# Where the sums of the next 512 rows are made and split, and eight reorderings around it, in a two-layer retention and window-attention kernel

## The reference

```python
# layer 0: retention, 4 heads, qk 256 wide, v and gate 512 wide, chunks of 64 rows
h = x @ w_in; q, k, v, g = split(h); q, k = rope(q), rope(k) * 256 ** -0.5
att = einsum(q, k) * decay_mask; inner = att @ v
cross = (q @ state) * xi; state = state * g_chunk + (k * zeta).T @ v
r = normalise(inner + cross)                      # per head, over 512
x = post_norm(x, (silu(g) * r) @ w_out)           # z = alpha * x + out, LayerNorm
# layer 1: window attention, 16 heads of 64, 4 shared key/value heads
k, v = split(x @ w_kv); q, gate = split(x @ w_in)
sc = q @ k.T * 64 ** -0.5 + bias_table[bucket]    # 64 queries against 128 keys
m = max(sc.max(-1), sink); p = exp(sc - m)
p = p / (p.sum(-1) + exp(sink - m)); o = p @ v
x = post_norm(x, (o * silu(gate)) @ w_out)
```

## Time and profile before

| | us |
|---|---|
| median of three runs | 2528.77 |
| the profiled execution, whole | 2527.57 |
| its span, first to last instruction | 2525.5 |
| PE busy in it | 2357.0 (93%) |
| DVE, ACT, POOL busy | 1901.5, 1115.1, 387.7 |
| granted PE clock, mean share of full | 0.972 |

### The profile page before, as it was taken

How to read it: one execution, slowest core, us unless ns; L and a number is a source line. 1 busy time by engine, 2 the same in 40 slices (tenths; PEclk the granted TensorE clock), 3 DMA queues, 4 the chain that set the end, 5 groups by cost and what they waited for, 6 DMA issues and landing times.

```text
span 2525.5 us, 30597 instructions
## 1 busy us (share of the span) xinstructions
PE 2357.0 (93%) x11506; PEld 1913.7 (76%) x11506; DVE 1901.5 (75%) x2693; ACT 1115.1 (44%) x1306; POOL 387.7 (15%) x376
## 2 busy tenths in 40 slices
PE   6799989899999999989999999998999999999995
PEld 5577777777778888777777888777777888878774
DVE  6787878768886668866797766884789667787577
ACT  2333444334544445523544444442454445553353
POOL 4122111132101110021200011102120110010032
PEclk9799999999999999989999999999999999999998
DMA  8776766571554444743274544574246344464413
GB/s 297 258 277 243 252 237 229 188 261 56 196 186 151 130 137 165 260 134 115 75 243 130 165 150 133 165 261 142 67 142 224 98 145 159 125 199 125 136 54 114
DMA packets 211602, 430.77 MB, mean 171 GB/s; under 512 B 14656, under 2 KB 52048, under 8 KB 207872
## 3 DMA queue, kind: packets, MB, share of 16 engines
q1 hardware_dynamic: 195648, 356.70, 43.5%
q0 software_dynamic: 15808, 72.12, 7.9%
HBM read 373.45 MB, written 51.12 MB: 168 GB/s over the span
## 4 chain that ended last, share of the span: by engine, by line
PE 59%; DVE 18%; issue 10%; DMA 7%; ACT 4%; POOL 2%; SPq 1%; POOLq 0%; DVEq 0%; ACTq 0%
PE accs L624 16%; PE accs L625 15%; PE accs L626 15%; DVE w_lo L1211 5%; DMA stage<-t_prep 3%; PE bank L624 3%; PE bank L626 2%; PE bank L625 2%; ACT w_hi L921 2%; DMA stage<-ret_w_in 2%; DMA t_prep<-t_buf 1%; PE bank L838 1%; PE bank L857 1%; PE bank L847 1%; DMA stage<-swa_w_in 1%
## 5 line engine op out<-in xcount | busy, mean ns | idle before, releaser
L1211 DVE TENSOR_TENSOR w_lo<-stage,w_hi 128x1024 fp32r<-128x1024 f32 x536 | 667.2, 1250 | 434.6 <-ACT w_hi L921 426.9
L921 ACT ACTIVATE w_hi<-stage 128x1024 fp32r<-128x1024 f32 x536 | 562.7, 1056 | 626.7 <-DMA stage<-t_prep 277.9
L624 PE MATMUL accs<-w_hi,xs 128*128 128x512 f32 x1120 | 449.3, 401 | 44.1 <-DVE w_lo L1211 11.9
L626 PE MATMUL accs<-w_hi,xs 128*128 128x512 f32 x1120 | 441.3, 394 | 0.0
L625 PE MATMUL accs<-w_lo,xs 128*128 128x512 f32 x1120 | 441.1, 394 | 0.0
L624 PEld LDWEIGHTS accs<-w_hi,xs 128*128 128x128 f32 x1120 | 213.2, 190 | 98.8 <-issue 43.8
L1763 POOL TENSOR_TENSOR rstd<-ve,half 128x1 f32<-128x1 f32 x96 | 80.7, 841 | 1264.2 <-DVE ve L1252 1216.4
L624 PE MATMUL accs<-x_hi,w_hi 128*128 128x512 f32 (+1 forms) x640 | 248.7, 389 | 17.8 <-DVE kT L1624 17.8
L626 PEld LDWEIGHTS accs<-w_hi,xs 128*128 128x128 f32 x1120 | 213.1, 190 | 46.0
L625 PEld LDWEIGHTS accs<-w_lo,xs 128*128 128x128 f32 x1120 | 213.5, 191 | 42.3
L625 PE MATMUL accs<-x_lo,w_hi 128*128 128x512 f32 (+1 forms) x640 | 240.0, 375 | 0.0
(11 more groups left out here) (185 smaller groups left out, 3940.1 us busy)
## 6 DMA issues: line engine op xcount, KB each, us to landing
stage<-t_prep SPq DMA_DIRECT2D x224, 512.0 KB, 4.5
stage<-ret_w_in SPq DMA_DIRECT2D x96, 512.0 KB, 3.9
stage<-ret_w_in SPq DMA_DIRECT2D x128, 256.0 KB, 2.9
stage<-swa_w_in SPq DMA_DIRECT2D x64, 512.0 KB, 4.1
t_prep<-t_buf POOLq DMA_DIRECT2D x28, 1024.0 KB, 8.0
stage<-ret_w_out SPq DMA_DIRECT2D x48, 512.0 KB, 3.6
cs<-rope_t SPq DMA_DIRECT2D x16, 1024.0 KB, 7.4
t_buf<-ret_w_in POOLq DMA_DIRECT2D x32, 512.0 KB, 9.9
```

Source lines behind the costliest of these rows:

```text
L624: mm(dst, lhs[0], rhs[0], start=start, stop=False, skip_group_check=reopened)
L626: return mm(dst, lhs[1], rhs[0], start=False, stop=stop, skip_group_check=reopened)
L921: copy(w_hi[:, g % HS], stage[:, g % LS], ACT.Copy).then_inc(w_hi_made, 1)
L1211: nc.vector.tensor_tensor(w_lo[:, g % LS], stage[:, g % LS], w_hi[:, g % HS].bitcast(F32), sub).then_inc(w_split, 1)
```

## The change

All four sums of the next block are now loaded by POOL as before (`load_part`, RO+15 to RO+24), but added by DVE at the end of pair KV, split by ACT and DVE at pairs Q0 to Q0+3 (`next_sum_hi`, `next_sum_lo`) and stored by SP as hi and lo, two DMAs for each sum, at Q0+1 to Q0+4. At pair 0 of the next block SP loads the eight halves straight into `xs`; nothing is split in head 0 any more (but in block 0). Beside that:

- the key copies stand at KV+2 instead of KV+3, and ahead of `make_hi`/`make_lo` of two pairs;
- two LayerNorm tiles are interleaved (`ln_two_tiles`), at RO+24 ahead of that pair's `make_lo`; at KV-1 `make_lo` follows `turn_x1_lo(0)`; the sums of P4 move from KV-1 to KV;
- the state of the last head is updated half before the statistics, and PE turns tile 1 of it in the middle of pair RO+4;
- in so, `output_sums` stands ahead of `split_so` (up to SO+8);
- scores are negated (query scale, bias and sinks times -1): DVE takes the minimum, ACT does exp(-x + lowest) as four instructions of 128x129, each with its own bias and a running sum, in place of one of 128x516; DVE's subtraction of the maximum and its row sums go;
- the spread of the bias table by DMA moves from ahead of the loop to pair 30; six sets of weight sums are loaded and made later in `T_PLAN`.

```diff
-T_PLAN = [(0, 0, -1, 1), (1, 1, -1, 1), (2, 2, -1, 2), (3, 3, -1, 2), (4, 0, 6, 9), (5, 1, 6, 11), (6, 2, 7, 13),
+T_PLAN = [(0, 0, -1, 1), (1, 1, -1, 1), (2, 2, -1, 2), (3, 3, -1, 2), (4, 0, 8, 11), (5, 1, 9, 13), (6, 2, 10, 14),
...
+                    if s > 0 and p == 0:
+                        sp.wait_ge(products, used(s * NP - 1))
+                        wait_sums_stored(sp, s)
                         for n in range(4):
-                            sp.dma_start(x_sums_next[:, n], x_sums_dram[n]).then_inc(sums_loaded[n], 16)
+                            for hl in range(2):
+                                sp.dma_start(xs[:, X_SUM_SLOT[n], hl].bitcast(F32), x_sums_dram[n, hl])\
+                                    .then_inc(sums_loaded[n], 16)
+                    if s + 1 < NS and Q0 + 1 <= p <= Q0 + 4:
+                        n = p - Q0 - 1
+                        sp.wait_ge(sums_split, 4 * s + n + 1)
+                        if s > 0:
+                            sp.wait_ge(sums_loaded[n], 32 * s)
+                        sp.dma_start(x_sums_dram[n, 0], sum_hi[n % 2][:].bitcast(F32))\
+                            .then_inc(sums_stored[n % 2], 16)
+                        sp.dma_start(x_sums_dram[n, 1], parts_lo[SUM_PART[n]][:].bitcast(F32)).then_inc(sums_stored[n % 2], 16)
...
+                    if p == RO + 4 and j == 0:
+                        turn_r(RH * s + RH - 1, 1)
+                    pe.wait_ge(state_ready, 8 * H + 7)
+                if t == 2:
                     pe.wait_ge(state_ready, 8 * (H + 1))
...
-                        turn_r(H - 1, 1)
                         turn_r(H - 1, 2)
...
+            def next_sum_hi(s, n):
+
+                act.wait_ge(parts_summed, s + 1)
+                if n == 0:
+                    act.wait_ge(scored, 16 * (s + 1))
+                if n > 1:
+                    act.wait_ge(sums_stored[n % 2], 64 * s + 32)
+                copy(sum_hi[n % 2][:], parts[SUM_PART[n]][:], ACT.Copy).then_inc(sums_hi, 1)
...
                 act.wait_ge(turned, 4 * H + t + 1)
                 copy(rT[:, 4 * h:4 * h + 4, t * P:(t + 1) * P],
...
-                    if p == KV + 3:
-                        act.wait_ge(products, full(s, p, 0))
+                        act.wait_ge(products, full(s, KV + 3, 0))
...
                         make_hi(g + AHEAD)
+                        make_hi(g + AHEAD + 1)
+                    if s + 1 < NS and Q0 <= p < Q0 + 4:
+                        next_sum_hi(s, p - Q0)
...
-                            act.wait_ge(p_shifted, NU * s + k + 1)
+                            act.wait_ge(lowest_ready, NU * s + k + 1)
+                            need(act, p_inv, NU * s + k)
+                            for i in range(4):
+                                scores = pr[:, k % 3, i, 0:BAND + 1]
+                                exped = copy(scores, scores, ACT.Exp, bias=lowest[:, i:i + 1], scale=-1.0,
+                                             accum_out=rsum[:, i:i + 1])
+                            exped.then_inc(p_exped, 1)
...
+            def sum_parts(s):
+
+                dve.wait_ge(parts_loaded, 64 * (s + 1))
+                a11, s3, a12, s2 = (x[:] for x in parts)
+                link(nc.vector.tensor_tensor(s3, a11, s3, sub))
+                link(nc.vector.tensor_tensor(s2, s2, s3, sub))
+                nc.vector.tensor_tensor(a11, s2, a11, add)
+                nc.vector.tensor_tensor(a12, a12, s2, sub).then_inc(parts_summed, 1)
+
+            def next_sum_lo(s, n):
+
+                dve.wait_ge(sums_hi, 4 * s + n + 1)
+                nc.vector.tensor_tensor(parts_lo[SUM_PART[n]][:], parts[SUM_PART[n]][:],
+                                        sum_hi[n % 2][:].bitcast(F32), sub).then_inc(sums_split, 1)
...
+            def ln_two_tiles(s, w, t):
+
+                dve.wait_ge(gb_loaded, 32 * (2 * s + w + 1))
+                ln_begin(s, w, t)
+                ln_gain(t)
+                ln_begin(s, w, t + 1)
+                ln_bias(s, w, t)
+                ln_gain(t + 1)
+                ln_bias(s, w, t + 1)
...
-                link(nc.vector.tensor_reduce(mx[:], x[:, :, 0:BAND + 1], AX.X, ALU.max))
-                nc.vector.tensor_tensor(x[:, :, 0:BAND + 1], x[:, :, 0:BAND + 1],
-                                        mx[:].unsqueeze(2).to_broadcast([P, 4, BAND + 1]), sub).then_inc(p_shifted, 1)
+                    link(nc.vector.tensor_scalar(x[:, :, 0:CHUNK], x[:, :, 0:CHUNK], -NEG_INF, None, add))
+                nc.vector.tensor_reduce(lowest[:], x[:, :, 0:BAND + 1], AX.X, ALU.min).then_inc(lowest_ready, 1)
...
             def softmax_back(s, u):
-                link(nc.vector.tensor_reduce(rsum[:], x[:, :, 0:BAND + 1], AX.X, add))
...
-                                split_x_sum(s, 3)
-                        if s > 0 and h == 0 and v in (1, 2, 4, 6):
...
                     if p == KV - 1:
                         turn_x1_lo(s, 0)
-                    if RO <= p < KV:
+                        make_lo(g + AHEAD)
+                    if RO <= p < KV - 1:
                         output_sums(s, "ro", p)
                     if p == RO + 24:
-                        ln_tile(s, 0, 0)
+                        ln_two_tiles(s, 0, 0)
+                        make_lo(g + AHEAD)
                     if p == KV:
                         turn_x1_lo(s, 1)
-                        ln_tile(s, 0, 2)
-                        ln_tile(s, 0, 3)
+                        output_sums(s, "ro", KV - 1)
+                        ln_two_tiles(s, 0, 2)
...
                         turn_x1_lo(s, 3)
+                        if s + 1 < NS:
+                            sum_parts(s)
...
-                    if p == KV + 3:
-                        dve.wait_ge(products, full(s, p, 1))
+                    if p == KV + 2:
+                        dve.wait_ge(products, full(s, KV + 3, 1))
...
                         make_lo(g + AHEAD)
+                        make_lo(g + AHEAD + 1)
+                    if s + 1 < NS and Q0 <= p < Q0 + 4:
+                        next_sum_lo(s, p - Q0)
...
+                    if SO <= p < SO + 9:
+                        output_sums(s, "so", p)
                     for n in SO_SPLITS.get(p, ()):
                         split_so(s, n)
...
-                    if SO <= p:
+                    if SO + 9 <= p:
...
+            def load_part(s, n):
-                for n, (u, i) in enumerate(((0, 0), (0, 1), (1, 0), (1, 1))):
-                    pool.dma_start(parts[n][:], x_turned[:, 4 * u:4 * u + 4, s * SB + i * HT:s * SB + (i + 1) * HT])\
-                        .then_inc(parts_loaded, 16)
+                wait_sums_stored(pool, s - 1)
+                u, i = divmod(n, 2)
+                pool.dma_start(parts[n][:], x_turned[:, 4 * u:4 * u + 4, s * SB + i * HT:s * SB + (i + 1) * HT])\
+                    .then_inc(parts_loaded, 16)
...
-            pool.wait_ge(bias_copied, 1)
-            pool.dma_start(bias_rep.rearrange("(h q n) -> h q n", q=CHUNK, n=NREL),
-                           brow[:].unsqueeze(1).to_broadcast([HEADS, CHUNK, NREL])).then_inc(bias_spread, 16)
...
+                    if p == 30 and s == 0:
+                        pool.wait_ge(bias_copied, 1)
+                        pool.dma_start(bias_rep.rearrange("(h q n) -> h q n", q=CHUNK, n=NREL),
+                                       brow[:].unsqueeze(1).to_broadcast([HEADS, CHUNK, NREL])).then_inc(bias_spread, 16)
...
-                        if p == RO + 18:
-                            load_parts(s + 1)
-                        if p == Q0:
-                            sum_parts(s + 1)
-                        if p == Q0 + 2:
-                            store_sums(s + 1)
+                        if p in (RO + 15, RO + 18, RO + 21, RO + 24):
+                            load_part(s + 1, (p - RO - 15) // 3)
```

148 lines of the change are left out of this document (73 added, 75 removed), and 2 rows, old and new, of the table T_PLAN.

## The result

The changed kernel took 2480.76 us (median of 4 runs, 2479.94 to 2483.47) against 2525.87 for the kernel before (4 runs, 2521.13 to 2528.85): a ratio of 0.9823, 95% interval 0.9804 to 0.9843. The forecast was 2474 in a range of 2450 to 2502. The direction and the size were right to 7 us; the sum was right partly because errors of its terms cancel.

What follows compares the result with a forecast made beforehand. The prediction took PE as the bound in the long stretches, with recurring waits and half-speed clock windows after long ones. Its terms summed to -54.3 us, giving 2474 us in a range of 2450 to 2502.

Steps and rivals of the forecast that it cites:

- Head 0: Head 0 of blocks 1 to 3: PE's 4.82 us wait for att_lo becomes two shorter ones, -9.6 us in all.
- no wait over 3 us: Sign for the profile after: in head 0 PE has no wait over 3 us, two of about 2.
- LayerNorm and kv: Pair 99 and kv: interleaved tiles bring x_lo earlier, -7.4 us in blocks 1 to 3 and -2.7 in block 0.
- predicted waits for w_lo of pair 99: Pair 99: PE newly waits about 2 us (1.3 to 2.1) for weights now made behind the LayerNorm tiles.
- First q pairs: First q pairs: earlier key copies end PE's wait for kT, 24.1 us gone and 4 given back, -20.1 us.
- what is late next are the key moves: First attention step: behind SP's stores the key moves cost PE 1 us in blocks 1 and 2, 2 in block 0.
- at nothing: DVE's four additions and the part_lo splits in q pairs cost nothing; without cover up to +1 us per block.
- so: The so stretches: output_sums ahead of one split shortens PE's waits for z, -4.5 us.
- Softmax: Attention gates: DVE's saved work hides under PE and ACT's four small exps fit its free time, 0 us.
- 0.75 us for each small exp: Attention gates: the limit up to which ACT's free time absorbs the four small exps at no cost.
- Start of block 0: Start of block 0: moving the bias spread and weight sums ends waits for w_lo and att_lo, -10 us.

Runs made afterwards that it cites:

- loads_spread: The changed kernel with the eight loads of half sums spread, two at each of pairs 0 to 3, instead of all at pair 0; ratio 0.9795.
- keys_only: The kernel before with only the key copies of ACT and DVE moved to KV+2, ahead of the weights of two pairs; 2515.32 us, ratio 0.9963.
- w99_first: The changed kernel with DVE's w_lo of pair 99 back ahead of the two interleaved LayerNorm tiles; 2489.15 us, ratio 0.9860.
- qt_first: The changed kernel with ACT's and DVE's qT copies ahead of the last split of the sums instead of behind it; 2476.41 us.
- more_exps: The changed kernel with eight more small exps on ACT per attention unit, results unused, ahead of the four; 2633.54 us, ratio 1.0432.

## Why the prediction was right, and where it was not

**Head 0** (forecast -9.6). Measured -13.6 in head 0. The mechanism held at each step: loads of 1.29 us each, weights late, a new wait at krT, att_lo early, the clock back. Its price was off: the two new waits were 1.4 each in blocks 1 and 2, not 2.3 and 1.7, and left no low clock at all behind them, where half was kept. In block 3 krT was 4.11, against the sign "no wait over 3 us", with a granted clock of 0.65 behind it. loads_spread shows the delay of the eight loads to be worth 1.4, 1.8 and 4.9 us.

**LayerNorm and kv** (-10.1). Measured -8.1 in pair 99 and kv: -7.6 in blocks 1 to 3, where -7.4 was forecast, and -0.5 in block 0 for -2.7. Of the -8.1 some 1.4 can be scatter, for keys_only has that much in these stretches without an edit to them. In its block 1 a wait of 3.2 us in all, as before, left a granted clock of 0.75 over 6.8 us, where before had 0.58. The predicted waits for w_lo of pair 99 came, 1.98, 1.14 and 1.91 us; w99_first shows that the exchange itself is even.

**First q pairs** (-20.1). This step failed. Its first half was exact: 24.1 us gone, shown by the edit alone. The second half, "what is late next are the key moves", was not: 23.4 us came back, not 4. In blocks 1 and 2 the cause is what the prediction never priced, the order on DVE: `part_lo` stands ahead of qT, takes 1.25 us, and waits 1.43 more through ACT for the landing of a store. Without these two PE's 3.43 would have been 0.75 (qt_first has 0.85), which also leaves the clock up. The prediction had put down the splits "at nothing" under the q pairs' 5.44 us and looked at their length, not at what they wait for and what stands behind them; qt_first takes 10 of those 11.4 us back (5 by the lowest values of the same code). In block 0 ACT stands 9.84 us for a load of weights amid POOL's and SP's transfers. keys_only gives back 10.8 us there without the sums' edits, but by another wait, a sum of weights whose load is late. Moving 1 MB away gives 4.7 (2.5 of it lost again in the gates), and the rest stays open.

**so** (-4.5). Measured -0.2. Of the seven waits of the earlier trace rows one stands in each so stretch, 2.40 us at P6. It fell to 1.18, but one of 1.34 came at P7:

```profile
1239.01 0.47 PE L644 MATMUL accs<-w_hi,xs 128*128 128x512 f32 x1 [1.18 <-DVE z L1452]
...
1251.75 0.47 PE L644 MATMUL accs<-w_hi,xs 128*128 128x512 f32 x1 [1.34 <-DVE z L1452]
```

DVE is without a gap in this stretch, so a split put behind z only comes in front of the next z. The step took a reordering for less work.

**Softmax** (0). The gates took 74.25 us for 74.02: right. The bound behind it was wrong: 0.75 us for each small exp came from ACT's free time, with 15 units for 12, and more_exps shows a loop through DVE and ACT to bind with ACT 83% busy.

**Start of block 0** (-10). Measured -16.8 in its four heads, from one profile of each kernel. By the 376.6 us of keys_only and the 364.2 to 372.2 of the kernels with the change it is anything from 4 to 22. The 8.9 us for w_lo, the larger part of the forecast, is not in the profile of keys_only at all (its longest there is 2.6), so that row was in part chance. The reason was the other one: the plan of weight sums gives 10 to 13, the spread of the bias table nothing that can be told. POOL's stand of 7.77 us did fall to 2.46, as forecast. Naming the 30 us DMA as the cause was the most striking row, not the right one.

**The sum.** -54.3 forecast, -44.3 measured. The q step missed by 19.4, `so` by 4.3 and kv by 2; heads, start of block 0 and what nobody forecast (heads 1 to 3 of blocks 1 to 3, -4.4) gave 16 back. That the sum came out is luck to that extent.

## What to carry to other kernels

When a step is moved onto an engine's list, price three things: its length, the latest thing it waits for, and the first critical thing that stands behind it; a split of 1.25 us cost PE 5.3 here: its length, the 1.4 it stood waiting, and the low clock behind PE's wait. A loop through two engines can bind while both have free time: add up the way from one unit to the next, not each engine's busy time. A long wait hides the next one, so make the edit alone and see what comes back. A reordering on an engine without gaps moves a wait, it does not remove it.

## What the hardware showed unexpected

- Running sums are instructions: each exp with `accum_out` is followed by a read of 0.188 us. It overlaps the exp before it and the one behind it by 0.1 us each, so the 0.393 us exps start 0.386 apart. Copies on ACT without such a read start 0.10 before the one ahead ends (1103.02 + 1.06, the next at 1103.98), so a read takes some 0.09 us of ACT.
- Two waits of 1.4 us left the granted clock at 1.00, one of 3.4 had 0.58 in the 6.8 us behind it. The same 3.0 to 3.2 us at the first kv pair had 0.58 in one block and 0.75 in two others of the kernel before.
- The same load of 512 KB landed in 3.9, 9.3, 12.0 or 12.2 us by what was issued ahead of it and beside it, and the same stores cost PE as much from POOL's queue as from SP's in blocks 1 and 2, though ACT then waited 6.36 us for a store and 1.13 for weights, where it had waited 1.59 and 6.30.
- Scatter is local: one stretch repeats within 0.1 us while ro, with the same code, moves by 6, and a q half with a wait in it by 2 to 3.
